# Recurrent heads of a two-layer decoder step: the spread of the maxima as a 128-row product behind the output gate, the state products in 32-column groups

## What is computed

```python
def step(carry, inp):                      # one chunk of tokens, all heads
    c, n, m = carry                        # matrix state (64 x 128), vector state, running maximum
    b = jnp.cumsum(lf, axis=-1)
    d = jnp.where(causal, b[..., :, None] - b[..., None, :] + li[..., None, :], -jnp.inf)
    inter = b + m[..., None]
    m_loc = jnp.maximum(inter, jnp.max(d, axis=-1))
    w_intra = jnp.exp(d - m_loc[..., None])
    w_inter = jnp.exp(inter - m_loc)
    sw = jnp.einsum('bhtd,bhsd->bhts', qc, kc) * w_intra
    num = w_inter[..., None] * jnp.einsum('bhtd,bhde->bhte', qc, c) + jnp.einsum('bhts,bhse->bhte', sw, vc)
    qn = w_inter * jnp.einsum('bhtd,bhd->bht', qc, n) + jnp.sum(sw, axis=-1)
    den = jnp.maximum(jnp.abs(qn), jnp.exp(-m_loc))
    hc = num / den[..., None]
    ...
    c_new = a[..., None, None] * c + jnp.einsum('bhs,bhsd,bhse->bhde', w, kc, vc)
```

## Time and profile before

| | |
|---|---|
| median of 3 runs | 1271.58 us (1270.91 to 1271.8) |
| the profiled execution | 1270.95 us, of which the span (first to last instruction) 1269.2 us |
| PE busy / PEld busy | 1242.3 us (98%) in 8929 matmuls / 1217.6 us (96%) |
| DVE / ACT / POOL busy | 737.7 us (58%) / 582.5 us (46%) / 96.2 us (8%) |
| chain that ended last | PE 92%, DVE 3%, ACT 1%, DMA 1% |
| granted clock of TensorE, mean | 0.997 |
| DMA | 200.50 MB, 158 GB/s |

### The profile page before, as it was taken

The page is one execution under the profiler, slowest core; times in us unless marked ns, Lnnn a source line. Parts: engine busy times, 40 slices in busy tenths (PEclk is TensorE's granted clock), DMA queues, the critical chain, the costliest instruction groups (busy, mean ns, idle before and its releaser), DMA issues.

```text
span 1269.2 us, 22196 instructions
## 1 busy us (share of the span) xinstructions
PE 1242.3 (98%) x8929; PEld 1217.6 (96%) x8929; DVE 737.7 (58%) x1156; ACT 582.5 (46%) x918; POOL 96.2 (8%) x117
## 2 busy tenths in 40 slices
PE   6999999999999999999999999999999999999996
PEld 6999999999889999999999999999996899999996
DVE  7565655565787655554555565654556576565433
ACT  7454533443455554533334554533443465454332
POOL 3000001100323000000000000000020110000011
PEclk9999999999999999999999999999999999999998
DMA  8434244633434444334543744334567743433441
GB/s 303 166 132 165 101 137 153 206 125 124 136 123 148 160 158 139 138 114 159 179 166 133 241 147 151 136 114 144 184 232 287 282 162 133 165 133 123 137 137 41
DMA packets 35994, 200.50 MB, mean 158 GB/s; under 512 B 4362, under 2 KB 6538, under 8 KB 20450
## 3 DMA queue, kind: packets, MB, share of 16 engines
q1 hardware_dynamic: 33858, 192.34, 43.7%
q0 software_dynamic: 2080, 7.39, 1.8%
HBM read 193.14 MB, written 6.57 MB: 157 GB/s over the span
## 4 chain that ended last, share of the span: by engine, by line
PE 92%; DVE 3%; issue 1%; ACT 1%; DMA 1%; SPq 0%; POOL 0%; POOLq 0%; DVEq 0%; ACTq 0%
PE bank L429 30%; PE bank L431 30%; PE bank L430 30%; DMA raw<-vc_in 1%; DVE cn L1495 0%; PE bank L539 0%; ACT junk L1059 0%; DMA raw<-w_in 0%; PE bank L550 0%; DVE dmat L1450 0%; PE bank L489 0%; DVE x L1729 0%; PE bank L761 0%; ACT dmat L1052 0%; DVE w_lo L1244 0%
## 5 line engine op out<-in xcount | busy, mean ns | idle before, releaser
L429 PE MATMUL bank<-h_hi,w_hi 128*128 128x320 f32 x1920 | 597.5, 311 | 11.5 <-DVE h_lo L1256 10.5
L431 PE MATMUL bank<-h_hi,w_lo 128*128 128x320 f32 x1920 | 594.1, 309 | 0.0
L430 PE MATMUL bank<-h_lo,w_hi 128*128 128x320 f32 x1920 | 594.1, 309 | 0.0
L919 ACT ACTIVATE w_hi<-raw 128x1024 fp32r<-128x1024 f32 (+1 forms) x368 | 335.8, 959 | 458.4 <-PE bank L431 454.2
L1244 DVE TENSOR_TENSOR w_lo<-raw,w_hi 128x1024 fp32r<-128x1024 f32 (+1 forms) x368 | 392.9, 1109 | 117.9 <-ACT w_hi L919 117.8
L429 PEld LDWEIGHTS bank<-h_hi,w_hi 128*128 128x128 f32 x1920 | 361.2, 188 | 14.1 <-DVE w_lo L1244 10.4
L430 PEld LDWEIGHTS bank<-h_lo,w_hi 128*128 128x128 f32 x1920 | 361.3, 188 | 0.4
L431 PEld LDWEIGHTS bank<-h_hi,w_lo 128*128 128x128 f32 x1920 | 361.2, 188 | 0.0
L430 PE MATMUL bank<-f_lo,w_hi 128*128 128x320 f32 x704 | 216.5, 308 | 0.0
L429 PE MATMUL bank<-f_hi,w_hi 128*128 128x320 f32 x704 | 216.5, 307 | 0.0
L431 PE MATMUL bank<-f_hi,w_lo 128*128 128x320 f32 x704 | 216.5, 307 | 0.0
(11 more groups left out here) (208 smaller groups left out, 616.5 us busy)
## 6 DMA issues: line engine op xcount, KB each, us to landing
raw<-w_in SPq DMA_DIRECT2D x88, 1024.0 KB, 4.8
raw<-w_out SPq DMA_DIRECT2D x64, 704.0 KB, 4.1
raw<-w_a SPq DMA_DIRECT2D x12, 1024.0 KB, 4.8
raw<-w_kv SPq DMA_DIRECT2D x8, 1024.0 KB, 4.8
raw<-vc_in SPq DMA_DIRECT2D x16, 512.0 KB, 6.4
raw<-kc_in SPq DMA_DIRECT2D x12, 512.0 KB, 4.7
raw<-w_oa SPq DMA_DIRECT2D x4, 1024.0 KB, 5.2
raw<-w_q SPq DMA_DIRECT2D x4, 1024.0 KB, 4.8
```

The costliest lines, as they stand in the source:

```text
L429: pe.matmul(out, wh, mh, start=first, stop=False)
L430: pe.matmul(out, wh, ml, start=False, stop=False)
L431: return pe.matmul(out, wl, mh, start=False, stop=last)
L919: sc.activation(w_hi[:, n_at % 2, part * w:part * w + w], raw[:, raw_of(n_at) % RAW, part * w:part * w + w], ACT.Copy).then_inc(hi_done, 1)
```

## The change

Three things change, all in the recurrent heads.

1. `sel` and `neg_hl` get 128 rows instead of 40. The added rows are zero, and `spread_maxima` is a product with the whole array. It moves behind `o_chunk`, and runs two heads ahead: `spread_maxima(1)` behind `o_chunk(0)`, `spread_maxima(h + 2)` behind `o_chunk(h + 1)`.
2. The prompt's state products (L655) are cut into four groups of 32 columns instead of two of 64: twice as many matmuls, each of half the columns of keys.
3. DVE's and ACT's orders in the loop over heads are rewritten: `decay(h + 1)` and `spread_queries(h + 1)` come before `denominators(h)`, the exponential before the squares; `weights(h + 1)` stands before `variances(h)` for even h and behind it for odd h; `gate_half(h)` comes one step later, behind the split and ahead of `keep_gate(h + 1)`; at the last head `z_split(0)` and `z_split(1)` come before the denominators and the squares. `decay` waits for the weights of the head before.

```diff
--- before.py
+++ after.py
@@ -100,7 +100,7 @@
         con = sb("con", [128, C_COLS])
         row_room = sb("row_room", [128, R_COLS])
         row = row_room[0:8, :]
-        sel = sb("sel", [40, H, 128], f32r)
+        sel = sb("sel", [128, H, 128], f32r)
         par = sb("par", [128, P_COLS])
         wg = sb("wg", [128, KT, 40])
         epsc = sb("epsc", [128, 1])
@@ -124,7 +124,7 @@
                 cb = sb("cb", [8, T], f32, own)
                 cm = sb("cm", [8, T], f32, own)
                 neg = sb("neg", [8, 384], f32, own)
-                neg_hl = sb("neg_hl", [40, 384], f32r, own)
+                neg_hl = sb("neg_hl", [128, 384], f32r, own)
                 mt = sb("mt", [8, T], f32, own)
                 tmp = sb("tmp", [8, T], f32, own)
                 mo = sb("mo", [8, 1 + NB], f32, own)
@@ -651,9 +651,9 @@
                     pe.wait_ge(cp_done, (h + 1) // 2)
                 if h % 2 == 0:
                     for t in range(2):
-                        for g in range(2):
-                            pe.matmul(bank[2][64 * g:64 * g + 64, 0:DV], kw[:, t, (h + g) * 64:(h + g) * 64 + 64],
-                                      v_tok[:, t, h + g, 0:DV], start=(t == 0), stop=(t == 1),
+                        for a in range(4):
+                            pe.matmul(bank[2][32 * a:32 * a + 32, 0:DV], kw[:, t, h * 64 + 32 * a:h * 64 + 32 * a + 32],
+                                      v_tok[:, t, h + a // 2, 0:DV], start=(t == 0), stop=(t == 1),
                                       skip_group_check=True)
 
             def sample_states(h):
@@ -696,15 +696,16 @@
 
             units(U_A, P_A, 7, 8, h_wait=lambda kt: first_scores() if kt == KT // 2 else None)
             o_chunk(0)
+            spread_maxima(1)
             for h in range(H):
                 head_outputs(h)
-                if h + 1 < H:
-                    spread_maxima(h + 1)
                 sample_states(h)
                 if h + 1 < H:
                     if h % 2:
                         scores_of_two(h + 1)
                     o_chunk(h + 1)
+                    if h + 2 < H:
+                        spread_maxima(h + 2)
                 else:
 
                     pe.wait_ge(p_done, H)
@@ -1076,15 +1077,15 @@
             split_at(U_A + 9)
             tanh(0)
             for h in range(H):
-                head_squares(h)
                 if h + 1 < H:
                     decay(h + 1)
-                    head_scale(h)
                 else:
                     sc.wait_ge(unit_done, U_OA)
                     z_split(0)
                     z_split(1)
-                    head_scale(h)
+                head_squares(h)
+                head_scale(h)
+                if h + 1 == H:
                     for g in range(2, H):
                         z_split(g)
                 for k, part in HALVES.get(h, ()):
@@ -1446,6 +1447,8 @@
             def decay(h):
 
                 ve.wait_ge(head_n, h + 1)
+                if h >= 1:
+                    ve.wait_ge(p_done, h)
                 for t, (o, i) in enumerate((((0, 256), 0), ((256, 384), 128), ((384, 448), 256))):
                     ins = ve.scalar_tensor_tensor(
                         out=dmat[:, o[0]:o[1]], in0=bank[4][:, i:i + o[1] - o[0]], scalar=cols[:, t, h:h + 1],
@@ -1519,24 +1522,28 @@
             project(7)
             split_at(U_A + 9)
             keep_gate(0)
-            gate_half(0)
             for h in range(H):
-                denominators(h)
-                variances(h)
                 if h + 1 < H:
                     decay(h + 1)
                     spread_queries(h + 1)
-                    weights(h + 1)
-                    states(h)
-                    for k, part in HALVES.get(h, ()):
-                        split_half(U_A + k, U_A + k, part)
-                    keep_gate(h + 1)
-                    gated(h)
-                    gate_half(h + 1)
                 else:
                     z_split(0)
                     z_split(1)
-                    states(h)
+                denominators(h)
+                if h % 2 == 0:
+                    weights(h + 1)
+                variances(h)
+                if h % 2 and h + 1 < H:
+                    weights(h + 1)
+                states(h)
+                if h + 1 < H:
+                    for k, part in HALVES.get(h, ()):
+                        split_half(U_A + k, U_A + k, part)
+                    gate_half(h)
+                    keep_gate(h + 1)
+                    gated(h)
+                else:
+                    gate_half(h)
                     for g in range(2, H - 1):
                         z_split(g)
                     gated(h)
```

## The result

| | before | after |
|---|---|---|
| median of 5 runs | 1271.58 us (1270.91 to 1272.27) | 1277.76 us (1276.98 to 1279.21) |
| the profiled execution | 1270.95 us, span 1269.2 | 1276.98 us, span 1275.2 |
| PE busy | 1242.3 us (98%) | 1241.5 us (97%) |
| DVE / ACT / POOL busy | 737.7 / 582.5 / 96.2 us | 738.4 / 583.2 / 98.9 us |

What follows compares the result with a forecast made beforehand. PE bounds the heads, DVE nearly; reordered DVE rounds (326.35 + 40.65 + 8.2 + 2.35 = 377.55, against 370.38) bring PE to the last head 6.5 us later: 1270.95 + 6.5 = 1277.45, median 0.63 above, 1278.1; range 1272.6 to 1280.3.

Steps and rivals of the forecast that it cites:

- ring and contention: Main case: slower DVE-POOL-ACT-DVE rounds in the heads, plus kwm slowing DVE; last turn 6.5 us later, 1278.1 us, 51%.
- PE bounds, but the margin is thin: In the heads PE waits once, 1.0 us; DVE's round is 7.45 us a head against PE's mean of 7.22.
- PE's terms: Shape changes saved and added on PE: -4 x 0.20 - 7 x 0.17 + 0.2 = -1.8 us; -2.8 without the wait.
- The spread product: Leaves the middle of PE's small products: one shape change of two goes, 0.17 us in 7 heads.
- The first spread product: On 128 rows it cannot share its start with the scores, adding a shape change: 0.2 us, bounds 0 and 0.4.
- The ring: DVE's round from w_lo through var, POOL and ACT back to w_lo: 8.13 us a head, where DVE took 7.45.
- The wait in front of `w_lo`: DVE idles before w_lo for ACT's w_hi: about 1.7 us in even heads, 1.4 in odd.
- `kwm`: POOL's 0.63 us falls inside DVE's w_lo: 0.47 us a head in heads 1 to 5, bounds 0 and 0.63.
- The start: Head 1's denominators on DVE come 0.7 us later, at 326.35 for 325.67.
- PE's side decides: Rival: DVE's waits go and PE's -2.8 us count, if the round is under PE's 6.97 us; 1268.8 us, 9%.
- The case without contention: Rival: DVE's longer round in the heads, but kwm misses w_lo: 4.15 us slower, 1275.7 us, 27%.
- The fall of the clock: Rival: PE's standstill at the last head lowers its clock for 36 large matmuls, 5 us more, 1283, 4%.

Runs made afterwards that it cites:

- e3: Changed kernel with ACT's copy of the half weight unit (w_hi) moved ahead of head_scale: 1268.31 us, ratio 0.9976.
- e7: e3 with the prompt's state products (L655) back in two groups of 64 columns: 1269.08 us, +0.77 over e3.
- e6: Kernel before the change, with only ACT's w_hi copy moved ahead of head_scale: 1271.17 us, ratio 0.9999.
- e4: Changed kernel with POOL's kwm for head h + 2 made right behind the power of head h: 1275.91 us, ratio 1.0032.
- e1: PE's edits of the change alone, with DVE's and ACT's head loops of the kernel before: 1271.97 us, ratio 1.0008.
- e10: Changed kernel with DVE's dmat, qm and pmat back behind var and ACT's exponential back behind the squares: 1273.57 us, ratio 1.0016.
- e8: e3 with sel and neg_hl back at 40 rows, the spread product in its new place: 1270.77 us, +2.46 over e3.
- e9: Changed kernel with ACT's w_hi copy ahead of head_scale in heads 1 to 3 only: 1272.71 us, ratio 1.0014.
- e2: DVE's and ACT's orders of the change, with PE's program and the 40 rows of the kernel before: 1281.05 us, ratio 1.0076.

## Why the prediction was right

The forecast was 1278.1, the result 1277.76, and the case that I gave 51%, ring and contention, is the one that the trace shows. Step by step:

- **PE bounds, but the margin is thin.** Right, and the hinge of it all: in e3, where DVE's round is short enough, PE's savings count in full; in the change they count for nothing.
- **PE's terms.** L655: 0.20 four times, 0.8; e7 gives 0.77. The spread product: in head 0 the small products took 2.94 us before and take 2.59 now, with L604's own time in both: 0.35 less, for a forecast of 0.20 + 0.17. The first spread product, priced +0.2, costs nothing: it starts at 308.65 and the scores at 309.01, but these then take 1.09 for 1.25, and the next large product starts at 310.03 in both kernels. That term was mis-sized, inside its bounds. -2.8 for PE's side with the wait gone against the -2.86 of e6 to e3.
- **The ring.** Head 2 to head 3, `w_lo` to `w_lo`, is 347.72 - 339.15 = 8.57 us, forecast 8.13 + 0.47 = 8.60. Its parts: `w_lo` 1.35 (1.13 forecast), gate_half 0.66 (0.25), keep_gate 0.40 (0.40), `gated` 0.46 (0.62), `dmat` and `qm` 1.25 (1.3), first denominator to `var` 1.44 (1.45), `var` to `w_lo` 3.01 (2.98). The last, the chain through POOL and ACT that was put together from gaps of two different heads, is within 0.03 and is the link that decides: e3 shortens it and the ring is gone.
- **The wait in front of `w_lo`.** There in all six heads, 1.57, 1.20, 1.57 in even ones (1.7 forecast) and 1.26, 1.25, 1.25 in odd ones (1.4). No wait is left before `pmat`, as forecast.
- **`kwm`.** The size was near, the place partly wrong. I put all of it on `w_lo`, "longer than 1.5 us in heads 1 to 5"; it is so in head 1 alone (1.95). In heads 2 to 5 `w_lo` takes 1.43, 1.30, 1.22, 1.30, and gate_half behind it 0.73 for 0.32. Together 0.73 + 0.62 + 0.49 + 0.41 + 0.49 = 2.74 us, forecast 2.35, and e4 gives 2.66. POOL's start was right: `kwm` begins 3.33 us behind `cn` in head 2 and 2.60 in head 3 (forecast 3.33 and 2.71), inside `w_lo`. What I had left out is that `kwm` itself can be stretched: it takes 1.46 in head 2 and 1.54 in heads 3 and 5, for 0.63, runs over the end of `w_lo`, and gate_half pays the rest.
- **The start.** Head 1's denominators at 325.88 for 326.35: I hadn't passed on to DVE that o_chunk(1) ends 0.36 earlier, PE's own saving in head 0. The rest of the sum from there was 50.93 for 51.2. Then 3.53 for 3.5 to the turn. The delay of the last turn was 5.77 us for 6.5, and the execution's 6.03. That the medians come within 0.3 of the forecast is in part luck, since small errors went opposite ways: the ring without contention was put too long (e4's six rounds take 48.23 us, forecast 48.85) and the contention too short; 0.26 us more were lost behind the last turn, and the median lies 0.78 above the profiled execution, for 0.63.
- **The rivals.** "PE's side decides" named 1268.8 and a point: a ring under PE's head. e3 goes under it and runs 1268.31. The case without contention named 1275.7; e4 runs 1275.91, with executions from 1274.4 to 1278.17, so this closeness is partly luck too. The fall of the clock did not come in the change's profile, and did in e4's.

What had not been seen is the next bound on the far side. With PE's edits and the old place of `dmat`, `qm` and `pmat`, PE waits for `c0` (1.5 us in e1, 2.1 in e10), and in e1 for `h_lo` only 0.7; in e3, whose `cn` comes early, it waits for neither.

## What to carry to other kernels

When work is moved out from behind an instruction, ask what it was covering: here a chain over two other engines, 2.98 us long, whose length could be added up before, from rows in which `w_lo` waits for nothing. If an order on one engine is tightened, look at the order on the engines that feed it; swapping two instructions of ACT, free by itself, turned a loss of 6.2 us into a gain of 3.0. And in this stage a matrix product padded to the shape of its neighbours beats a smaller one in a shape of its own, by 2.46 us for seven of them (e8).

## What was not expected of the hardware

**The clock fell after a short wait in one execution, and not in another.** e4's profiled execution, by stretch (length, busy time and count of PE, PEld, DVE, ACT, POOL, then the granted clock, DMA share, GB/s):

```profile
372.00:376.00 4.00, 4.00 (x22) 2.13 (x20) 2.77 (x12) 2.07 (x9) 0.17 (x1) 1.00 0.74 262
376.00:380.00 4.00, 2.43 (x8) 0.82 (x8) 3.05 (x10) 2.67 (x8) 1.30 (x2) 0.81 0.19 70
380.00:384.00 4.00, 4.00 (x16) 4.00 (x17) 3.01 (x5) 2.36 (x3) 0.00 (x0) 0.50 0.00 0
384.00:388.00 4.00, 4.00 (x25) 4.00 (x24) 2.60 (x6) 0.10 (x1) 1.03 (x2) 0.83 0.63 213
```

PE had waited 1.57 us for `ot` at 377.67 and run small products, its weight loads busy 0.82 of 4 us; then the granted clock is 0.50, 1.2 GHz for 2.4, until 385. The large matmuls show it, 0.47 us long and 0.27 apart, 0.31 and 0.15 at the higher level:

```profile
380.18 0.47 PE L430 MATMUL bank<-h_lo,w_hi 128*128 128x320 f32 x1
380.44 0.47 PE L431 MATMUL bank<-h_hi,w_lo 128*128 128x320 f32 x1
```

This execution took 1278.17 us at a mean clock of 0.993; two of the same kernel with a mean clock of 0.997 took 1274.4 and 1274.67, some 3.6 less (my rival said 5). e9 has one of 0.993 too, 1276.41 us, and one of 0.946, 1275.52, for a median of 1272.71; neither has a trace. The change's profile has the same wait of 1.58 at the same place, and stayed at 1.00. The Trainium skill, page TensorE: Matmul & The Clock Gate, Part 1, says that activity holds the higher clock; e4's fall behind a wait agrees with it. Why the change's profile shows none behind the same wait is not shown.

**DVE and POOL slow each other, and who pays changes from head to head.** The change's profile, heads 1 and 3:

```profile
330.33 1.95 DVE L1245 TENSOR_TENSOR w_lo<-raw,w_hi 128x1024 fp32r<-128x1024 f32 x1 [1.26 <-ACT w_hi L920]
330.57 0.63 POOL L1783 TENSOR_TENSOR kwm<-kw,con 64x256 f32<-64x256 f32 x1
...
347.72 1.30 DVE L1245 TENSOR_TENSOR w_lo<-raw,w_hi 128x1024 fp32r<-128x1024 f32 x1 [1.25 <-ACT w_hi L920]
347.95 1.54 POOL L1783 TENSOR_TENSOR kwm<-kw,con 64x256 f32<-64x256 f32 x1
```

In head 1 `kwm` starts 0.24 after `w_lo`, takes its usual 0.63, and `w_lo` 1.95 for 1.22. In head 3 (and alike in head 5) it starts 0.23 after `w_lo`, and now `kwm` takes 1.54 and `w_lo` 1.30. In head 2 it starts 0.44 after `w_lo`, and both are longer, 1.46 and 1.43. e2 repeats all of these lengths within 0.01. The Trainium skill, page SBUF — State Buffer, section Who interferes with whom, says that such a pair shares a port, held by one of them at a time, and that the order of issue decides who blocks. Heads 3 and 5 agree with it, since there the one that came second waited; head 1 doesn't, since there the one that came first paid, and head 2 does only in part. What makes head 1 differ from head 3 is not shown, and a start or a length on POOL is rough in this profile.
